# Third buffers in a mixture-of-experts stage, with a loop of three experts on TensorE

## The reference

```python
def expert_block(args):
    xr, e = args
    h = jax.nn.silu(xr @ w_gate[e]) * (xr @ w_up[e])      # 1024 -> 512
    return h @ w_down[e]                                   # 512 -> 1024
yb = lax.map(expert_block, (xb, blk_e)).reshape(P, D)
y = jnp.zeros((T, D), F32).at[tok_pad].add(yb.astype(F32) * gate_pad[:, None])
# afterwards: layer_norm(DN_ALPHA * x + hier_moe(x))
```

## Time and profile before

| | us |
|---|---|
| runs | 1838.14 (median), 1840.77, 1835.23 |
| the profiled execution | 1831.85 |
| its span, first to last instruction | 1830.1 |
| TensorE busy in it | 1732.0 (95%) |
| VectorE busy | 746.0 (41%) |
| ScalarE busy | 326.1 (18%) |
| GpSimd busy | 293.5 (16%) |

### The profile page before, as it was taken

One profiled execution on the slowest core, in us unless ns is written; L12 is line 12 of the kernel. 1 busy time (PEld: TensorE's weight loads), 2 busy tenths in 40 slices (PEclk: granted clock), 3 DMA queues, 4 the chain that ended last, 5 costly groups with the idle time before them and its releaser, 6 DMA issues. The chain is left out here.

```text
span 1830.1 us, 34543 instructions
## 1 busy us (share of the span) xinstructions
PE 1732.0 (95%) x15263; PEld 1085.3 (59%) x15263; DVE 746.0 (41%) x1174; ACT 326.1 (18%) x741; POOL 293.5 (16%) x291
## 2 busy tenths in 40 slices
PE   8999999999999999999998999849999999999976
PEld 4565556645666644445666665536666666666642
DVE  1213456514766753310104333564434443344337
ACT  1212224401334210110002111000111110111116
POOL 2100000001322000000000000043333333333223
PEclk9999999999999999999999999769999999999997
DMA  8951011001002041253100000549999999999957
GB/s 276 310 187 47 1 45 51 1 1 49 1 5 98 5 161 35 73 195 115 46 26 32 24 23 12 192 156 391 420 422 421 422 420 421 422 422 416 391 219 276
DMA packets 66230, 330.70 MB, mean 181 GB/s; under 512 B 14948, under 2 KB 17352, under 8 KB 53088
## 3 DMA queue, kind: packets, MB, share of 16 engines
q1 hardware_dynamic: 47856, 280.70, 38.5%
q0 software_dynamic: 12192, 26.76, 4.0%
q10 hardware_dynamic: 6096, 22.02, 3.9%
HBM read 288.05 MB, written 50.23 MB: 185 GB/s over the span
## 5 line engine op out<-in xcount | busy, mean ns | idle before, releaser
L864 PE MATMUL psum<-arena 128*32 128x256 f32 x6144 | 339.8, 381 | 20.1 <-issue 13.3
L864 PEld LDWEIGHTS psum<-arena 128*32 128x32 f32 x6144 | 230.6, 111 | 127.9 <-issue 33.1
L461 PE MATMUL psum<-arena 128*128 128x512 f32 x640 | 282.2, 600 | 2.9 <-issue 2.9
L1468 DVE COPY arena<-psum 128x512 f32<-128x512 f32 (+6 forms) x128 | 83.8, 663 | 368.0 <-PE psum L461 201.2
L461 PEld LDWEIGHTS psum<-arena 128*128 128x128 f32 x640 | 121.9, 193 | 149.9 <-issue 149.5
L684 PE MATMUL psum<-arena 128*128 128x352 f32 x576 | 177.9, 460 | 0.0
L873 PE MATMUL psum<-arena 128*32 128x256 f32 x3072 | 172.3, 379 | 0.5 <-DVE arena L1920 0.5
L446 PE MATMUL psum<-arena 128*128 128x352 f32 x576 | 170.8, 460 | 0.1
L1178 ACT ACTIVATE arena<-psum 128x128 f32<-128x128 f32 (+7 forms) x193 | 94.1, 497 | 344.8 <-PE psum L439 243.8
L2131 POOL DMA_INDIRECT arena<-x_rows,consts x102 | 103.8, 1017 | 282.8 <-DVE arena L1923 254.0
L873 PEld LDWEIGHTS psum<-arena 128*32 128x32 f32 x3072 | 116.3, 110 | 50.1 <-DVE arena L1920 1.0
(11 more groups left out here) (279 smaller groups left out, 1653.0 us busy)
## 6 DMA issues: line engine op xcount, KB each, us to landing
arena<-in_moe_w_down SPq DMA_DIRECT2D x34, 2048.0 KB, 21.4
arena<-in_moe_w_gate SPq DMA_DIRECT2D x34, 2048.0 KB, 14.5
arena<-in_moe_w_up SPq DMA_DIRECT2D x34, 2048.0 KB, 21.1
y_blocks<-arena ACTq DMA_DIRECT2D x1, 20736.0 KB, 102.2
arena<-in_w_in SPq DMA_DIRECT2D x6, 2048.0 KB, 9.8
arena<-in_x_prompt SPq DMA_DIRECT2D x9, 512.0 KB, 3.3
arena<-in_w_out SPq DMA_DIRECT2D x2, 2048.0 KB, 8.1
arena<-in_xa_wk SPq DMA_DIRECT2D x2, 2048.0 KB, 11.9
```

The costliest lines, as they stand in the source:

```text
L461: last = mm(ps[0:n, c * 512:(c + 1) * 512], lhs(k), rhs(k)[:, c * 512:(c + 1) * 512], start=(k == 0), stop=(k == KD - 1))
L864: last = mm(out, xeT[:, b, a, k, :], gu[b][:, :, k, j * P:(j + 1) * P], start=(k == 0), stop=(k == KD - 1))
L1468: take(V.tensor_copy(out, src), key)
```

## The change

- A third buffer for expert weights, at columns 24576 to 36863 of the arena. It lies over `x1`, so the normed rows are lost in the expert stage; SP reads them back from `x2_dram` for the tail, and DVE waits for that (x1_back).
- `xeT`, `hhT`, the gate-up banks `B_U` and the gate rows have three buffers instead of two; `B_Y` has one pair of banks instead of two pairs; `ye` has three buffers instead of four; `xe` keeps two.
- TensorE's loop runs three experts a turn over experts 2 to 31; steps 2 and 31 are no longer written out. SP's loop has three experts a turn; DVE's and ACT's have six.
- SP loads the weights of expert 2 ahead of the stage, behind waits for the last norm, the stores of x2 and the last turned rows; from then on it loads expert e after gate-up and down of expert e-3.
- POOL waits for places_stored ahead of the loads of the third norm's parameters, which have moved.

```diff
-        EXP = [0, 12288]
+        EXP = [0, 12288, 24576]
...
-        xeT = view(R + 11264, "a s k t", a=2, s=NS, k=KD, t=32)
+        xeT = view(R + 13312, "a s k t", a=3, s=NS, k=KD, t=32)
-        hhT = view(R + 14336, "a s k t", a=2, s=NS, k=KE, t=32)
+        hhT = view(R + 16000, "a s k t", a=3, s=NS, k=KE, t=32)
-        ye = [view(R + a, "s n", s=NS, n=256) for a in (15360, 16128, 21504, 22272)]
+        ye = [view(R + 17152 + 768 * a, "s n", s=NS, n=256) for a in range(3)]
...
         # TensorE
-            B_U = [psum[:, a * BANK:(a + 2) * BANK] for a in (0, 2)]
-            B_Y = [psum[:, a * BANK:(a + 2) * BANK] for a in (4, 6)]
+            B_U = [psum[:, a * BANK:(a + 2) * BANK] for a in (0, 2, 4)]
+            B_Y = psum[:, 6 * BANK:8 * BANK]
...
-            def step(e, b, j, first=False):
-
+            def step(e, r, turn_n, first=False):
+
+                s, before_s = r % 3, (r - 1) % 3
                 if not first:
                     pe.wait_ge(xt_ready, e + 1)
-                pe.wait_ge(wg_in[b], 16 * j + 16)
-                pe.wait_ge(wu_in[b], 16 * j + 16)
-                if not first:
-                    wait_count(pe, h_ready, e - 1)
-                gate_up(b, first).then_inc(gu_done, 1)
+                pe.wait_ge(wg_in[s], 16 * (turn_n + r // 3) + 16)
+                pe.wait_ge(wu_in[s], 16 * (turn_n + r // 3) + 16)
+                gate_up(s, first).then_inc(gu_done, 1)
                 if not first:
                     pe.wait_ge(h_ready, e)
-                    pe.wait_ge(wd_in[1 - b], 16 * (j + b))
-                    if not isinstance(e, int) or e > 2:
-                        pe.wait_ge(y_ready, e - 2)
-                    down(1 - b).then_inc(y_done, 1)
+                    pe.wait_ge(wd_in[before_s], 16 * (turn_n + (r - 1) // 3) + 16)
+                    if not isinstance(e, int) or e > 1:
+                        pe.wait_ge(y_ready, e - 1)
+                    down(before_s).then_inc(y_done, 1)
 
             step(0, 0, 0, first=True)
             step(1, 1, 0)
-            step(2, 0, 1)
-            with pe.Fori(1, NE // 2 - 1) as i:
-                step(2 * i + 1, 1, i)
-                step(2 * i + 2, 0, i + 1)
-            step(NE - 1, 1, NE // 2 - 1)
+            with pe.Fori(1, NE // 3 + 1) as i:
+                for r in range(-1, 2):
+                    step(3 * i + r, r, i)
             pe.wait_ge(h_ready, NE)
-            pe.wait_ge(wd_in[1], 16 * (NE // 2))
-            pe.wait_ge(y_ready, NE - 2)
-            down(1).then_inc(y_done, 1)
+            pe.wait_ge(wd_in[(NE - 1) % 3], 16 * ((NE - 1) // 3) + 16)
+            pe.wait_ge(y_ready, NE - 1)
+            down((NE - 1) % 3).then_inc(y_done, 1)
...
         # SP
             sp.dma_start(gu[0][:, 1], up_w[0]).then_inc(wu_in[0], 16)
+            sp.wait_ge(ln_ready, 2 * NT)
+            sp.wait_ge(x2_stored, 16 * NT)
+            emptied(sp, ("X2T", NT - 1))
+            sp.dma_start(gu[2][:, 0], gate_w[2]).then_inc(wg_in[2], 16)
+            sp.dma_start(gu[2][:, 1], up_w[2]).then_inc(wu_in[2], 16)
+            sp.dma_start(wd[2], down_w[2]).then_inc(wd_in[2], 16)
...
-            def load_gate_up(e, b, done):
-                sp.wait_ge(gu_done, done)
+            def load_gate_up(e, s):
+                sp.wait_ge(gu_done, e - 2)
...
+            load_gate_up(3, 0)
+            load_gate_up(4, 1)
+            load_down(3, 0)
+            with sp.Fori(1, NE // 3) as i:
+                for r in range(2, 5):
+                    load_gate_up(3 * i + r, r % 3)
+                    load_down(3 * i + r - 1, (r - 1) % 3)
+            load_down(NE - 1, (NE - 1) % 3)
...
+            sp.wait_ge(y_done, NE - 2)
+            sp.dma_start(x1[0:DEC, 8, :], x2_dram[SEQ:T, :]).then_inc(x1_back, 16)
+            sp.dma_start(x1[:, 0:8, :], x2_dram[0:SEQ, :].rearrange("(t p) n -> p t n", p=P)).then_inc(x1_back, 16)
...
         # DVE
+            for e in range(7):
+                dve_expert(e, e, 0)
+            with dve.Fori(1, (NE - 2) // 6) as i:
+                for r in range(1, 7):
+                    dve_expert(6 * i + r, r, 3 * i)
+            dve_expert(NE - 1, NE - 1, 0, last_one=True)
...
             dve.wait_ge(ln3_loaded, 32)
+            dve.wait_ge(x1_back, 32)
...
         # POOL
                 if e == 2:
+                    pool.wait_ge(places_stored, 1)
                     for i, n in enumerate(("ln3_g", "ln3_b")):
```

More of the change, by code:

```diff
@@ L278, in build @@
         places_ready, row_ready = sem("places_ready"), sem("row_ready")
-        wg_in, wu_in, wd_in = ([sem(f"{n}_in{i}") for i in range(2)] for n in ("wg", "wu", "wd"))
+        wg_in, wu_in, wd_in = ([sem(f"{n}_in{i}") for i in range(3)] for n in ("wg", "wu", "wd"))
+        x1_back = sem("x1_back")
         xe_in = [sem(f"xe_in{i}") for i in range(2)]
         x0_in, x0_ready = [sem(f"x0_in{i}") for i in range(NS)], sem("x0_ready")
-        y_out = [sem(f"y_out{i}") for i in range(4)]
+        y_out = [sem(f"y_out{i}") for i in range(3)]
         gu_done, y_done = sem("gu_done"), sem("y_done")
@@ L1107, in _, with load_down @@
             sp.dma_start(gu[0][:, 1], up_w[0]).then_inc(wu_in[0], 16)
+            sp.wait_ge(ln_ready, 2 * NT)
[4 more added lines that the diff above has]
+            sp.dma_start(wd[2], down_w[2]).then_inc(wd_in[2], 16)
             def dyn(w, e):
                 return w[bass.ds(e, 1)].rearrange("a p k n -> (a p) k n")
-            def load_gate_up(e, b, done):
-                sp.wait_ge(gu_done, done)
[L1114 to L1129, removed]
+            def load_gate_up(e, s):
+                sp.wait_ge(gu_done, e - 2)
+                sp.dma_start(gu[s][:, 0], dyn(gate_w, e)).then_inc(wg_in[s], 16)
+                sp.dma_start(gu[s][:, 1], dyn(up_w, e)).then_inc(wu_in[s], 16)
+            def load_down(e, s):
+                sp.wait_ge(y_done, e - 2)
+                sp.dma_start(wd[s], dyn(down_w, e)).then_inc(wd_in[s], 16)
+            load_gate_up(3, 0)
[6 more added lines that the diff above has]
+            load_down(NE - 1, (NE - 1) % 3)
             sp.wait_ge(tables_ready, 1)
@@ L1167, in _ @@
                 sp.wait_ge(state_out[i], 32 * HH // 2)
-            for i in range(4):
-                sp.wait_ge(y_out[i], 16 * NS * NE // 4)
+            for i in range(3):
+                sp.wait_ge(y_out[i], 16 * NS * Y_TURNS[i])
         @block.scalar
@@ L1370, in _ @@
             A(vals[:, 4, :], vals[:, 4, :], ACT.Exp).then_inc(route_exped, 1)
-            B_Y = [psum[:, a * BANK:(a + 2) * BANK] for a in (4, 6)]
+            B_Y = psum[:, 6 * BANK:8 * BANK]
             gate_rows = [psum[:, a * BANK:a * BANK + NS * 256].rearrange("p (s m n) -> p s m n", m=2, n=P)[:, :, 0, :]
-                         for a in (0, 2)]
+                         for a in (0, 2, 4)]
             def store_y(rows, slot, s):
@@ L1387, in y_rows @@
                 for a in range(NS):
-                    last = A(ye[slot][:, a, :], B_Y[b][:, a * 256:(a + 1) * 256], ACT.Copy, scale=gate2[:, b, a:a + 1])
+                    last = A(ye[slot][:, a, :], B_Y[:, a * 256:(a + 1) * 256], ACT.Copy, scale=gate2[:, b, a:a + 1])
                 last.then_inc(y_ready, 1)
@@ L1395, in act_step @@
                     act.wait_ge(h_ready, e)
-                A(sg, gate_rows[r % 2], ACT.Exp, scale=-1.0).then_inc(g_exp, 1)
+                A(sg, gate_rows[r % 3], ACT.Exp, scale=-1.0).then_inc(g_exp, 1)
                 if not isinstance(e, int) or e > 0:
-                    y_rows(e - 1, (r - 1) % 2, (r - 1) % 4, turn_n)
+                    y_rows(e - 1, (r - 1) % 2, (r - 1) % 3, turn_n + (r - 1) // 3)
             for e in range(7):
[L1401 to L1406, removed]
+                act_step(e, e, 0)
+            with act.Fori(1, (NE - 2) // 6) as i:
+                for r in range(1, 7):
+                    act_step(6 * i + r, r, 2 * i)
+            act_step(NE - 1, NE - 1, 0)
+            y_rows(NE - 1, (NE - 1) % 2, (NE - 1) % 3, (NE - 1) // 3)
             act.wait_ge(tables_ready, 1)
@@ L1424, in spilled @@
                 if isinstance(j, int):
-                    act.wait_ge(y_out[b], 16 * NS * NE // 4)
+                    act.wait_ge(y_out[b], 16 * NS * Y_TURNS[b])
                 for a in range(2):
@@ L1443, in _ @@
                             spilled(2 * i + b, b)
-            for i in range(4):
-                act.wait_ge(y_out[i], 16 * NS * NE // 4)
+            for i in range(3):
+                act.wait_ge(y_out[i], 16 * NS * Y_TURNS[i])
             A(rstd[:, 1:2], eps_ln, ACT.Copy).then_inc(fin_ready, 1)
@@ L1903, in _ @@
             V.tensor_copy(y_idx, none_q[:, 0:NE]).then_inc(places_stored, 1)
-            halves_of = [psum[:, a * BANK:a * BANK + NS * 256].rearrange("p (s m n) -> p s m n", m=2, n=P) for a in (0, 2)]
+            halves_of = [psum[:, a * BANK:a * BANK + NS * 256].rearrange("p (s m n) -> p s m n", m=2, n=P)
+                         for a in (0, 2, 4)]
             def silu_up(b, n):
```

(19 more changed lines are left out.)

15 lines of the change are left out of this document (8 added, 7 removed).

## The result

| | before | after |
|---|---|---|
| median, us | 1839.38 (4 runs) | 1897.82 (4 runs, 1893.71 to 1902.49) |
| profiled execution, us | 1831.85 | 1899.41 |
| its span, us | 1830.1 | 1897.6 |
| ratio | | 1.032 (95% interval 1.029 to 1.035) |

The changed kernel is 58 us slower by the medians and 67.5 by the two profiled spans. It was forecast at 1879 in a range of 1820 to 1915.

The account below looks back on a forecast made before the run. TensorE bounds most of the kernel; in the expert stage weight DMA costs it 18.9 us. Loop reloads of 58.5 less a gain of 18.1 (18.9 less 0.8) make 40.4 slower: 1838.1 + 40.4 = 1879 us, range 1820 to 1915.

Parts of the forecast that it names:

- The code is fetched anew: Likeliest case, chance 0.74: TensorE's three-expert loop does not stay on the engine; nine turns back cost 58.5 us.
- the paragraph behind it: TensorE's loop: eight 16 KiB blocks cannot hold eight touched plus one fetched ahead, so each turn back misses its first block.
- The third buffer: Expert stage: expert 2's 6.29 MB move into idle DMA time; gain between 14.9 us (weights bind) and 18.9 (TensorE binds).
- the code stays: Rival, chance 0.18: TensorE's loop stays on the engine, branches cost 0.21 us hidden; 14.1 us faster, 1824.
- One y bank: Expert stage: each down waits until ACT empties the previous one; only the last two downs lack cover, cost 0.8 us.
- the cover that the early loads left: Ahead of the expert stage: 3 us between expert 2's loads and expert 0's gather; priced 0, 4.7 us if lost.
- One sign: Expected in the profile after, expert stage: weights land later than now, since they wait for nothing; no size given.
- price per turn back: TensorE's loop: 4.8 us stall plus 1.7 us clock loss, 6.5 us together, for nine turns back.
- the branch: TensorE's branch closing the loop: between 3.77 us with idle DMA and 8.5 with full queues, 6.1 taken.
- the gap: TensorE's stall at each turn back, after 1.3 us of cover from queued matmuls: 2.4 to 7.2 us, 4.8 taken.
- the clock: TensorE's granted clock falls after each turn-back stall: 0 to 3.4 us lost, 1.7 taken.
- SP and POOL: Their added waits and the x1 read-back ahead of the tail: priced 0, with 43 us for 15 us of queue.

Follow-up runs that it names:

- experiment 2: Changed kernel with the first instruction of TensorE's loop placed at the start of a 16 KB code block; 1832.15 us, ratio 0.997. Same run as e2.
- experiment 3: Changed kernel with TensorE's loop starting at the 129th place of a 16 KB code block; 1908.53 us, one run. Same run as e9.
- Experiment 5: Kernel before, two weight buffers, with TensorE's loop running four experts a turn instead of two; 1881.91 us, ratio 1.025. Same run as e4.
- e5: Changed kernel with the loop's closing branch announced at each turn's head and the x1 read-back held behind the first spilled block's scatter; 1827.14 us, ratio 0.9945.
- e6: Changed kernel with TensorE's loop at a block's start and the x1 read-back held behind the first spilled block's scatter; 1823.69 us, ratio 0.992.
- e4: Kernel before, two weight buffers, with TensorE's loop running four experts a turn instead of two; 1881.91 us, ratio 1.025. Same run as Experiment 5.
- e8: As e5, but expert 2's weights are issued only after the first gate-up; 1839.44 us, ratio 1.001.
- e1: Changed kernel with TensorE's loop written out as thirty steps, no branch back; 1843.48 us, ratio 1.003.
- e2: Changed kernel with the first instruction of TensorE's loop placed at the start of a 16 KB code block; 1832.15 us, ratio 0.997. Same run as experiment 2.
- e7: Changed kernel with weight loads from expert 3 on cut to 64 columns of one k block of each matrix; 1862.59 us, one run.
- e3: Changed kernel with the loop's closing branch announced by an instruction at the head of each turn; 1836.40 us, ratio 0.999.
- e9: Changed kernel with TensorE's loop starting at the 129th place of a 16 KB code block; 1908.53 us, one run. Same run as experiment 3.
- e10: Kernel before with TensorE's loop at four experts a turn and its closing branch announced at each turn's head; 1858.81 us, one run.

## Why the prediction came out

**The direction was right, by a step whose reason was not the one that decided.** *The code is fetched anew* decided and could not be read from before; the packets, the branches, the gap before every third gate-up and none before the others came as listed, and experiments 2, 3 and 5 tie them to the loop's blocks. But the prediction took this side because the loop is half as long again, and length alone does not decide: the same 1743 instructions stay when they begin at a block's start (experiment 2). The count in the paragraph behind it, eight blocks touched and one fetched ahead, is what the runs bear out. Only, a loop of this length need not touch eight: 7.1 packets was a little high, at 256 instructions to a block it is 6.8, and seven can hold that. That the changed kernel's loop touches eight hangs on where the code ahead of it happens to end, which no row of before tells. In that the direction was in part luck.

The 18.9 us of *The third buffer* all came back, as was reckoned for a stage that TensorE bounds, but they do not show what the buffer gives. Experiment 5 gets them back with two buffers: there the stalls let the weights catch up. What the buffer itself is worth is seen where the stalls are gone: the thirty turns lose 4.7 us in e5 and 3.2 in e6, so of the 18.9 it gives back 14.2 and 15.7, which is near the 14.9 that were reckoned for a stage that the weights bound. The rival *the code stays* had 1824. The changed kernel with only its loop moved measured 1832.15, because the entry and the read-back, which that sum holds at nothing, are in it; that e6 with the late read-back measures 1823.69 is in part chance.

*One y bank* was put at 0.8 and cost 0.9. The gather of expert 0 landed in 3.07 us (3.03 before), so the cover that the early loads left it held. One sign did not come: the weights land sooner after their issue, not later (median of the gate loads 10.3 us, 14.5 before).

**The size was short by 18 us in the medians, in two terms.** The *price per turn back* was 6.5 us and measured 8.09, 72.8 instead of 58.5. The branch was nearly right (6.3 for 6.1) and so was the gap (47.6 / 9 = 5.3 for 4.8). What was mis-sized most is the clock: 72.8 - 47.6 = 25.2 us, 2.8 per turn, where 1.7 was taken as the middle of 0 and 3.4. The rows for the upper end were there; a stall of 5 us comes nearer to them than to none.

The step *SP and POOL* failed: the read-back was priced at 0, because DVE needs the rows 43 us later. It asked who waits for the transfer and not who else stands on the DMA engines meanwhile. The first spilled block's scatter did, ACT waited for that, and 6.5 us followed. The same sentence said that only 15 us of queue were needed; it landed after 29.2.

With both terms put right the sum is -18.9 + 72.8 + 0.9 + 6.5 = 61.3 us. The spans differ by 67.5, of which 5.8 lie ahead of the stage: 61.7. The medians are 58.4 apart; the profiled execution of before was 7.5 us below its median, that of after 1.6 above.

## What to carry to other kernels

A loop that grows is to be counted in blocks of code, from where it starts and with the block that is fetched ahead, before a buffer is added that makes it grow; where it is at the edge, its place or an announced branch costs one line and gave back over 60 us here. The deeper buffer at a saturated DMA gained here only what it moved into idle DMA time. A transfer that nobody waits for is priced by what it delays on the engines that it shares.

## What had not been expected of the hardware

TensorE's clock falls without a gap. Around 220 us all kernels run the same code, and TensorE is busy without a gap in the 10 us before. Yet the granted clock stayed at 1.00 in the profiled execution of before and fell to 0.50 in that of after, at 219.6 by the windows around it, for some 13 us. The same window of before and of after:

```profile
224.00:231.00 7.00, 6.54 (x51) 4.33 (x52) 5.68 (x15) 3.23 (x10) 0.00 (x0) 1.00 0.01 2
```

```profile
224.00:231.00 7.00, 7.00 (x28) 4.61 (x27) 3.83 (x9) 1.56 (x5) 0.00 (x0) 0.50 0.00 0
```

1.2 GHz for 2.4 costs after 5.2 us here. The profiled executions of the experiments have the same fall, for a time that differs: some 7 us in e4, e5, e6 and e8, 13 in e1, e2 and e7, 27 in e3, e9 and e10 (estimates, from the granted clocks of the windows of 218 to 262). In these last three the third gate-up starts 7.5 to 8.8 us later than in after. So a part of what two runs of one kernel differ by lies here, and two profiled spans are best compared stage by stage. Why the clock falls, and why for longer in some, is open.

And a jump's price follows the traffic: with the read-back running beside it, the branch over the unused loop of spilled experts took 5.75 us in e5 and 7.58 in e6 instead of the 3.77 of the earlier trace rows.
